# Inverse levels of a chunked scan taken head by head on one Trainium2 core, with the budgets of TensorE's filler pieces changed

## What is computed

```python
def step(s, inp):
    r_t, w_t, k_t, v_t, a_t, b_t = inp
    sa = jnp.einsum('bhvk,bhk->bhv', s, a_t)
    s = s * w_t[:, :, None, :] + sa[..., None] * b_t[:, :, None, :] + v_t[..., None] * k_t[:, :, None, :]
    return s, jnp.einsum('bhvk,bhk->bhv', s, r_t)
```

## Time and profile before

| | us |
|---|---|
| median of 3 runs (lowest, highest) | 2486.53 (2483.26, 2489.89) |
| the profiled execution | 2488.11 |
| its span, first to last instruction | 2486.3 |
| TensorE busy in it | 2415.5 (97%) |
| VectorE, ScalarE, GpSimd busy | 1338.3, 790.2, 748.4 |
| the scan, from the first full block of the first pair to the last pair | about 96 to 1020 |

### The profile page before, as it was taken

The page is one execution under the profiler, slowest core; times in us unless marked ns, Lnnn a source line. Parts: engine busy times, 40 slices in busy tenths (PEclk is TensorE's granted clock), DMA queues, the critical chain, the costliest instruction groups (busy, mean ns, idle before and its releaser), DMA issues.

```text
span 2486.3 us, 65623 instructions
## 1 busy us (share of the span) xinstructions
PE 2415.5 (97%) x28580; PEld 1775.9 (71%) x28580; DVE 1338.3 (54%) x2764; ACT 790.2 (32%) x1612; POOL 748.4 (30%) x730
## 2 busy tenths in 40 slices
PE   6999999999999998899999999999999999999998
PEld 1566666666666666658888888865558888875797
DVE  4766666666666665454563333834624434545553
ACT  3354544445454443221221121013510014022312
POOL 2533433343434442100001034400055400540381
PEclk9999999999999999899999999999999999999999
DMA  7111111111111113544336732220134444332343
GB/s 302 49 39 45 42 39 48 41 46 39 39 39 39 50 37 124 188 169 153 136 133 213 269 120 89 91 84 30 43 130 171 146 145 139 136 120 72 98 153 110
DMA packets 80148, 258.30 MB, mean 104 GB/s; under 512 B 11639, under 2 KB 16984, under 8 KB 79096
## 3 DMA queue, kind: packets, MB, share of 16 engines
q1 hardware_dynamic: 75304, 242.94, 28.5%
q0 software_dynamic: 1360, 5.89, 0.7%
q10 hardware_dynamic: 3200, 5.27, 0.6%
HBM read 253.02 MB, written 1.05 MB: 102 GB/s over the span
## 4 chain that ended last, share of the span: by engine, by line
PE 55%; DVE 2%; DMA 1%; ACT 0%; issue 0%; SPq 0%; DVEq 0%; ACTq 0%
PE ps L2327 9%; PE ps L2125 9%; PE ps L2050 9%; PE ps L1975 7%; PE ps L2180 4%; PE ps L2105 3%; PE ps L2376 2%; PE ps L2225 2%; PE ps L2393 1%; PE ps L1895 1%; PE ps L2245 1%; PE ps L2210 1%; PE ps L2265 1%; PE ps L2204 1%; DMA ring<-in_w_mods 1%; PE ps L2083 1%
## 5 line engine op out<-in xcount | busy, mean ns | idle before, releaser
L2050 PE MATMUL ps<-h,ring 128*128 128x256 f32 x1024 | 225.6, 379 | 0.0
L2050 PEld LDWEIGHTS ps<-h,ring 128*128 128x128 f32 x1024 | 193.9, 190 | 34.9 <-issue 9.9
L1053 ACT ACTIVATE general<-general 64x512 f32<-64x512 f32 x160 | 101.8, 636 | 164.8 <-DVE general L1252 162.2
L583 PE MATMUL ps<-general,ring 128*128 128x512 f32 x256 | 134.9, 623 | 0.8 <-issue 0.8
L3515 POOL TENSOR_TENSOR general<-h 128x1024 f32<-128x1024 f32 (+1 forms) x4 | 7.2, 1803 | 423.8 <-DVE general L3255 238.0
L599 PE MATMUL ps<-general,ring 128*128 128x512 f32 x256 | 134.1, 629 | 0.0
L774 PEld LDWEIGHTS ps<-general 64*64 64x64 f32 (+1 forms) x5120 | 77.5, 130 | 68.8 <-issue 44.9
L2180 PE MATMUL ps<-ring,h 128*128 128x512 f32 x256 | 110.2, 592 | 0.0
L2327 PE MATMUL ps<-general,ring 128*128 128x256 f32 (+1 forms) x576 | 106.3, 327 | 0.6 <-DVE general L3328 0.6
L3509 POOL TENSOR_TENSOR general<-general 128x256 f32<-128x256 f32 x16 | 12.7, 796 | 310.2 <-ACT general L2550 310.2
L1252 DVE STREAM_TRANSPOSE general<-general 128x512 f32<-128x512 f32 x160 | 104.3, 690 | 2.2
(11 more groups left out here) (440 smaller groups left out, 5329.7 us busy)
## 6 DMA issues: line engine op xcount, KB each, us to landing
ring<-in_w_mods SPq DMA_DIRECT2D x88, 512.0 KB, 4.4
ring<-in_w_feature SPq DMA_DIRECT2D x74, 512.0 KB, 3.2
ring<-in_w_rkvg SPq DMA_DIRECT2D x64, 512.0 KB, 3.7
ring<-in_w_in SPq DMA_DIRECT2D x48, 512.0 KB, 3.2
ring<-in_w_merge SPq DMA_DIRECT2D x48, 512.0 KB, 4.2
ring<-in_w_out SPq DMA_DIRECT2D x32, 512.0 KB, 6.5
ring<-in_w_token SPq DMA_DIRECT2D x24, 512.0 KB, 4.8
ring<-in_w_merge SPq DMA_DIRECT2D x48, 256.0 KB, 2.7
```

The costliest lines, as they stand in the source:

```text
L583: mm = pe.matmul(ps[:, 0, :], W.wt[:, 0, k, :], W.mix_k[:, k, :], start=(k == 0), stop=(k == KD - 1))
L1053: last = act.activation(W.U[g:g + 64, 1], W.X0[a:a + 64, 1], ACT.Copy)
L2050: mm = pe.matmul(ps[:, n % 4, 0:NX], weights(key, k), R.h[:, k, 0:NX], start=(k == 0), stop=(k == KD - 1))
```

## The change

The budgets become

```diff
-FILL_BELOW = (0, 1000, 1000, 1000, 1000, 500)
-FILL_GROWN = (0, 1200, 800, 500, 500, 1000)
+FILL_BELOW = (0, 2000, 1500, 1500, 1500, 500)
+FILL_GROWN = (0, 0, 0, 0, 0, 1000)
```

and the loops of `below` and `grow` take head h as the outer one, with semaphores and PSUM banks by head instead of by direction:

```diff
-    def below(l):
-        for j in range(4):
-            for h in range(2):
+    def below(i, l):
+        for h in range(2):
+            if l > 1:
+                pe.wait_ge(t_out[h], (LAST - 1) * i + l - 1)
+            for j in range(4):
                 for p in range(2):
                     a = oth(p)
                     for z in range(2):
-                        b0, g, q = 2 + 2 * z, solved_in(z, p), 4 * h + j
+                        bank, g, q = 2 + 2 * h + z, solved_in(z, p), 4 * h + j
...
-                        if (j, h, p) == (3, 1, 1):
-                            mm.then_inc(Z("y_done")[z], 1)
+            mm.then_inc(Z("y_done")[h], 1)
 
     def grow(i, l):
         for z in range(2):
-            pe.wait_ge(y_out[z], LAST * i + l)
             pe.wait_ge(u_out[z], 6 * i + l)
-        for j in range(4):
-            for h in range(2):
+        for h in range(2):
+            pe.wait_ge(y_out[h], LAST * i + l)
+            if l == LAST:
+                pe.wait_ge(y_out[1], LAST * (i + 1))
+            for j in range(4):
...
-                        if (j, h, p) == (3, 1, 1):
-                            mm.then_inc(Z("ty_done")[z], 1)
+            mm.then_inc(Z("ty_done")[h], 1)
```

```diff
+    def mask_level(i, h, l):
+        dve.wait_ge(Z("y_done")[h], LAST * i + l)
+        mask = W.lmask[:, l - 1, :, :].unsqueeze(2).broadcast_to([P, 2, 4, 32])
+        dve.tensor_tensor(W.Y[:, :, 4 * h:4 * h + 4, :], head_banks(h), mask, ALU.mult).then_inc(Z("y_out")[h], 1)
+
+    def add_level(i, h, l):
+        dve.wait_ge(Z("ty_done")[h], LAST * i + l)
+        for z in range(2):
+            dst = half_columns(W.T[:, z, 4 * h:4 * h + 4, :], l, z)
+            grown = head_banks(h)[:, z].rearrange("p q (b w) -> p q b w", w=1 << l)
+            last = dve.tensor_tensor(dst, dst, grown, ALU.add)
+        last.then_inc(Z("t_out")[h], 1)
...
             else:
-                dve.wait_ge(Z("t_out")[z], (LAST - 1) * i + l - 1)
+                for h in range(2):
+                    dve.wait_ge(Z("t_out")[h], (LAST - 1) * i + l - 1)
```

More of the change, by code:

```diff
@@ L773, in below @@
                             left, own = left[:, t:t + 32], slice(g + t, g + t + 32)
-                        mm = pe.matmul(ps[own, b0 + h, j * P:j * P + 32], left, right, start=True, stop=True)
-                        if (j, h, p) == (3, 1, 1):
-                            mm.then_inc(Z("y_done")[z], 1)
+                        mm = pe.matmul(ps[own, bank, j * P:j * P + 32], left, right, start=True, stop=True)
+            mm.then_inc(Z("y_done")[h], 1)
     def grow(i, l):
         for z in range(2):
-            pe.wait_ge(y_out[z], LAST * i + l)
             pe.wait_ge(u_out[z], 6 * i + l)
-        for j in range(4):
-            for h in range(2):
+        for h in range(2):
[3 more added lines that the diff above has]
+            for j in range(4):
                 for p in range(2):
@@ L786, in grow @@
                     for z in range(2):
-                        b0, g, q = 2 + 2 * z, solved_in(z, p), 4 * h + j
+                        g, q = solved_in(z, p), 4 * h + j
                         if l < LAST:
-                            mm = pe.matmul(ps[a:a + 64, b0 + h, j * P:j * P + 32], W.U[g:g + 64, z, q, :], W.Y[g:g + 64, z, q, :],
+                            mm = pe.matmul(ps[a:a + 64, 2 + 2 * h + z, j * P:j * P + 32], W.U[g:g + 64, z, q, :], W.Y[g:g + 64, z, q, :],
                                            start=True, stop=True)
@@ L794, in grow @@
                             own = slice(g + t, g + t + 32)
-                            mm = pe.matmul(ps[g + c:g + c + 32, b0 + h, j * P:j * P + 32], W.Y[own, z, q, :], W.U[own, z, q, t:t + 32],
+                            mm = pe.matmul(ps[g + c:g + c + 32, 2 + 2 * z + h, j * P:j * P + 32], W.Y[own, z, q, :], W.U[own, z, q, t:t + 32],
                                            start=True, stop=True)
-                        if (j, h, p) == (3, 1, 1):
-                            mm.then_inc(Z("ty_done")[z], 1)
+            mm.then_inc(Z("ty_done")[h], 1)
     def seen_values(i):
@@ L921, in pairs_pe @@
         for l in range(1, LAST + 1):
[L922 to L925, removed]
+            below(i, l)
             if l == LAST:
@@ L1225, in mask_tokens, with head_banks, add_last @@
             dve.tensor_tensor(W.Ax[:, z, h].rearrange("p (j q) n -> p j (q n)", q=2), src, mask, ALU.mult).then_inc(Z("xm_out")[z], 1)
[L1227 to L1233, removed]
-        grown = two_banks(2 + 2 * z)[:, :, 0:32]
[L1235 to L1243, removed]
+    def head_banks(h):
+        return ps[:, 2 + 2 * h:4 + 2 * h, :].rearrange("p z (j n) -> p z j n", n=P)[:, :, :, 0:32]
+    def mask_level(i, h, l):
[9 more added lines that the diff above has]
+        last.then_inc(Z("t_out")[h], 1)
+    def add_last(i, z):
+        for h in range(2):
+            dve.wait_ge(Z("ty_done")[h], LAST * i + LAST)
+        dve.wait_ge(Z("u_out")[z], 6 * i + LAST)
+        t = 32 - 32 * z
+        dst = W.U[:, z, :, t:t + 32]
+        grown = two_banks(2 + 2 * z)[:, :, 0:32]
+        dve.scalar_tensor_tensor(dst, grown, W.lmask[:, LAST - 1, 1 - z, 0:1], dst, ALU.mult, ALU.add).then_inc(Z("u_out")[z], 1)
     def turn_inverse(i, l):
@@ L1344, in pairs_dve @@
             turn_inverse(i, l)
-            for z in range(2):
-                mask_level(i, z, l)
+            for h in range(2):
+                mask_level(i, h, l)
             if l == 1:
@@ L1360, in pairs_dve @@
                 floor(m)
-            for z in range(2):
-                add_level(i, z, l)
+            if l < LAST:
+                for h in range(2):
+                    add_level(i, h, l)
+            else:
+                for z in range(2):
+                    add_last(i, z)
         if ahead:
```

## The result

The changed kernel takes 2542.32 us (median; 2538.53 to 2544.99), the kernel before took 2485.03 beside it: 1.0226 times as long [1.0206, 1.0247], 57 us slower. The profiled execution is the shortest of the four, 2538.53 with a span of 2536.7, against 2486.3 before. So the profiles differ by 50.4 us, 7 less than the medians, and what follows accounts for those 50.4. Every time in this part is the median of a kernel's executions; one execution of one experiment, 4888.75 us at a granted clock of 1.00, is set down as slow and is in no ratio.

The account below looks back on a forecast made before the run. Scan bound by TensorE's own work plus small waits; 4.04 us a pair gives 59.9 over fifteen pairs, last pair -3.6, clock +10: 66 us more, so 2553 us predicted; range 2515 to 2588.

Parts of the forecast that it names:

- Rivals 2: Only the state steps are paid; the three moved pieces find their data ready: 2499 us, chance 0.14.
- rival 4: Not slower: TensorE has hidden room in switches and weight loads, only savings stay: 2473 us, chance 0.04.
- The state steps, 5.73: Six advances, bound by round trips, keep 5.73 us without pieces; four formerly free pieces are paid elsewhere, 1.72 us a pair.
- g0 waits 1.6: Piece g0, now behind the first transitions, waits 1.6 us a pair for the values ScalarE copies after the solve.
- tv waits 0.7: Piece tv, now behind the growth of level 5, waits 0.7 us a pair for `v_raw`, holding the solve.
- `turn_out` waits 0.7: `turn_out`, now second at level 2, waits 0.7 us a pair for GpSimd's normalisation.
- The order by head, nothing: Four additions instead of two per level change nothing; bounds 0.1 us a level either side, 0.4 a pair.
- The clock, six falls of 1.7: Granted clock falls behind unfilled state steps in six of 15 pairs, 1.7 us each: +10 us, range 0 to +25.
- The last pair, -3.6: Early output weights' transfer chain starts 4.7 us earlier, but the waiting piece precedes level 4's `below`: -3.6 us.
- Rival 3: Zero budgets issue nothing; fewer switches, additions stand open, leftover pieces fill the state steps: 2487 us, chance 0.05.
- Theory I: In `first_blocks`, TensorE's instruction packets queue behind the gate weights' load; holding that load back saves 4 to 8 us.
- Rival S: Dense small products alone use up instructions faster than they come; stops stay despite holding the gate load, 2492 to 2495.

Follow-up runs that it names:

- the experiments with the values: Changed kernel with ScalarE's copy of the values moved before the four copies of the solve: 2524.26 us, ratio 1.0149.
- empty budgets: Changed kernel with a `fill` that returns at once on a budget of 0, so it takes no piece: 2510.1 us, ratio 1.0085.
- the late load: Gate weights' load (512 KB) held until the blocks are formed, added to the changed kernel with level 4's FILL_BELOW at 500: 2484.7 us, ratio 0.9989.
- idle products: Changed kernel with one unread 128x128 by 128x256 product in each of the four empty state steps: 2537.14 us, ratio 1.0207.

## Why the prediction was right, and where its steps were off

The side, the mechanism and the range held, the whole one (2515 to 2588) and the forecast's own (2540 to 2562): 2542 for 2553. Of the terms:

- **What binds the kernel**: held. Nearly every added wait or exposed piece reached the end; the experiments with the values and with the budgets show it from both sides. Weight loads were busy 568 of the 864 us (263.26 and 304.89 in the rows of the result), and that was no room in which the new waits could vanish. Rivals 2 (2499) and 4 (2473) fell with it. The point at which rival 4 would decide was worked out wrongly: savings of 0.68 a pair and 3.6 in the last outweigh up to 0.9 us of added wait a pair, not 0.25. It makes no difference, since 4.0 of the 4.7 added reached the end (3.3 net).
- **A budget of 0 takes one piece**: held; `grow` (L791) at 411.20 is followed by a piece at 412.21 in the timeline of after:

```profile
411.20 1.09 PE L791 MATMUL ps<-general 64*64 64x32 f32 x64
412.21 1.13 PE L583 MATMUL ps<-general,ring 128*128 128x512 f32 x2
413.27 1.14 PE L775 MATMUL ps<-general 64*64 64x32 f32 x64
```

- **The state steps, 5.73**: mis-sized, 5.24. The last advance is followed by the reads after 0.59 us (396.11 to 396.70), with a piece between them after 1.00 (608.86 to 609.86 before). The row of the last pair (5.90) was no better guide: the clock was low in it (0.55 from 1017), and the changed kernel's steps too take 5.67 where a fall lies in them. -0.5 a pair, -7 in all.
- **g0 waits 1.6**: 1.5 measured, 1.37 of it on the path. (The rows give 5.81 for the values, not 5.85.)
- **tv waits 0.7**: 0.5, 7.4 us in 15 times. **`turn_out` waits 0.7**: 0.34 from start to start in a middle pair. Both queues were the right ones. That the additions by head end earlier than assumed is the likely reason: with additions by direction the idle time at `turn_out` is 0.53 instead of 0.22. The levels as a whole are 0.35 a pair under the forecast.
- **The order by head, nothing**: right as an edit by itself, but worth 8 to 10 us under the new budgets. The prediction asked whether the piece behind the growth covers the additions, and took for granted that the move, the transposes and `turn_out` behind them end as before; under the new budgets `turn_out` waits for them, and there an earlier end counts.
- **The clock, six falls of 1.7**: six falls behind the fifteen walks; the five middle pairs that have one are longer by 7.7 us in all, three of them by 1.1, one by 1.7, one by 2.7. The size was taken from ten microseconds at 0.83; here the fall lies in the last waiting steps and the small products behind them, and costs less. Busy time and clock around the longest fall:

```profile
514.00:524.00 10.00, 9.02 (x129) 6.72 (x131) 7.21 (x17) 4.14 (x10) 1.82 (x2) 0.70 0.17 55
```

  The number of falls was a guess that came out by luck; nothing shown here says why some pairs have one and others none.
- **The last pair, -3.6**: -6.1 from its `first_blocks` on. The wait for `in_w_out` did not shrink to 4, it is gone: the transfer is still issued late, but the first early output comes later still, and what `turn_out` waits for costs 2.76 once. Sync engine and TensorE:

```profile
990.22 27.65 SPq L108 DMA_DIRECT2D ring<-in_w_mods  x7
1041.60 4.83 SPq L108 DMA_DIRECT2D ring<-in_w_out  x4
```
```profile
1032.52 0.41 PE L655 MATMUL ps<-eye,x 128*128 128x128 f32 x2 [2.76 <-issue]
1045.34 0.70 PE L1916 MATMUL ps<-general,ring 128*128 128x256 f32 x2
```

In sum the forecast was 15.6 us too high against the profile (66 for 50.4): 10 from the pair's 4.04 for 3.33, 2.5 from the last pair, 2.3 from the clock, the small rest mostly from stops of TensorE, of which the changed kernel has fewer (1.0 us for 2.6). Against the median (2542 for 2553) it was 11. Rival 3 has the time of empty budgets at 2487, and they took 2510: it asked where the pieces land and not which queue waits for them (ScalarE's copies of the values and the reads).

## What to carry to other kernels

Filler pieces have no price of their own, their place has one: moved ahead they wait for their inputs and hold all behind them, moved back they hold their consumer's queue, and the free places (round trips between engines) must stay filled. When budgets are cut in one place, write out the whole new list of pieces against places, and for each piece ask what it waits for and who waits for it. A change of order that measures nothing beside one set of budgets can be worth 8 to 10 us beside another.

## What the runs showed of the hardware

**TensorE can run out of instructions.** Where no semaphore held it, it stopped for up to 3.2 us within a group of equal products. A count over the traces ties these stops to the packets of its instruction queue. A packet holds 256 instructions (228 packets for 58,396 records of TensorE in the changed kernel). The fourteen kernels have 75 such stops of over 0.3 us between 92 us and 1080, and every one stands at the same place in the count of records modulo 256, where one packet's instructions end and the next one's begin. TensorE goes on 2.1 to 3.4 us after the packet's start, with a median of 2.4; and at none of the 2396 such borders of the fourteen kernels in this stretch does it go on sooner than 2.1 us. So the supply is what it waits for.

The traces also say why a packet comes too late. With two wide pieces fewer in the levels, the packets of the three long stops in `first_blocks` start 2.2 to 3.0 us after TensorE came to the border before, against a median of 0.9 in that kernel, while the gate's weights are in the DMA engines; with the late load the same three start after 0.9 to 1.2, and the long stops are gone. That is Theory I, and the late load took 9 us off one kernel and 6 off another. Inside the levels no load runs and the packet starts as usual, 1.0 to 1.3 us after, but TensorE is through with the 256 instructions before it in about 2.4 us, where the mean between packets is 5.7: there dense small products alone are enough, as Rival S has it, and those stops remain (4.7 us). The Trainium skill, page "Runtime: NRT & Kernel Launch", section "Instruction fetch mechanics", says that instructions are fetched in blocks of 16 KiB, which agrees with these packets, and calls the cost of a block mostly hidden; at most of the borders it was, but four stops of 2.6 us stand in the kernel before, and eleven of 10.9 in the one with nothing behind the growth and filled steps.

**The price of a lower clock depends on what stands behind it.** A fall behind mostly unfilled steps cost 1.1 us where small products followed, about 1.5 where twelve wide passes did. The four kernels with four unfilled steps had falls in five, three, nine and ten of the fourteen middle pairs; of the ten others, filled or with idle products, five had none and five had one or two. When a fall comes is irregular.
